# Four banks for the turned blocks of U, 16-bit index look-ups, ten gathered rows a tile in the expert layer of a hybrid decoder

## What is computed

```python
q = (ht @ w_query).reshape(T, 8, 2, 128)
s = einsum('thpd,hpnd->thpn', q, sub_keys)           # 8 heads x 2 halves x 128 keys
top_s, top_i = top_k(s, 16)
cand_s = top_s[:, :, 0, :, None] + top_s[:, :, 1, None, :]      # 16 x 16 sums
cand_i = top_i[:, :, 0, :, None] * 128 + top_i[:, :, 1, None, :]
fin_s, pos = top_k(cand_s.reshape(T, 8, 256), 16)
fin_i = take_along_axis(cand_i.reshape(T, 8, 256), pos, axis=-1)
gate = softmax(fin_s)
act = gelu(einsum('tkd,td->tk', expert_u[fin_i], x))             # 128 experts a token
out = einsum('tk,tkd->td', gate * act, expert_v[fin_i])
```

## Time and profile before

| | |
|---|---|
| median of 3 runs | 3357.28 us (3353.91 to 3363.41) |
| profiled execution | 3359.51 us |
| its span, first to last instruction | 3357.8 us |
| TensorE busy | 3265.7 us (97%) |
| VectorE busy | 2549.1 us (76%) |
| ScalarE busy | 900.3 us (27%) |
| GpSimd busy | 801.7 us (24%) |
| mean granted clock of TensorE | 0.985 of full speed |

### The profile page before, as it was taken

The page is one execution under the profiler, slowest core; times in us unless marked ns, Lnnn a source line. Parts: engine busy times, 40 slices in busy tenths (PEclk is TensorE's granted clock), DMA queues, the critical chain, the costliest instruction groups (busy, mean ns, idle before and its releaser), DMA issues. The chain is left out here.

```text
span 3357.8 us, 46048 instructions
## 1 busy us (share of the span) xinstructions
PE 3265.7 (97%) x17796; PEld 2872.9 (86%) x17796; DVE 2549.1 (76%) x5349; ACT 900.3 (27%) x1310; POOL 801.7 (24%) x625
## 2 busy tenths in 40 slices
PE   8999989899999999999999999999999999999998
PEld 7867755499999999999999999997888888888887
DVE  6611244322499999999989898876999999999996
ACT  4210301111122222224444444432222222222222
POOL 0000000000001100104333333342444444444440
PEclk9999989899999999999999999999999999999999
DMA  3010021311144444448889788889898898988883
GB/s 99 14 40 27 13 88 63 119 57 38 46 133 145 144 141 141 134 137 291 304 308 325 279 324 308 308 320 359 312 318 306 314 314 314 312 318 314 316 309 135
DMA packets 332962, 695.58 MB, mean 207 GB/s; under 512 B 34332, under 2 KB 194936, under 8 KB 326584
## 3 DMA queue, kind: packets, MB, share of 16 engines
q1 hardware_dynamic: 248600, 386.28, 33.0%
q0 software_dynamic: 84144, 306.35, 26.7%
HBM read 580.10 MB, written 110.64 MB: 206 GB/s over the span
## 5 line engine op out<-in xcount | busy, mean ns | idle before, releaser
L1782 ACT ACTIVATE up_a<-up_pa 128x384 f32<-128x384 f32 x256 | 126.0, 492 | 830.8 <-PE up_pa L1767 820.9
L1806 POOL DMA_INDIRECT lead<-in_peer_v_dram,idx x174 | 259.6, 1492 | 352.9 <-DVE acc_s L1825 326.7
L2478 DVE TENSOR_TENSOR acc<-pd_po,acc 128x512 f32<-128x512 f32 x384 | 264.6, 689 | 93.3 <-PE pd_po L2537 90.7
L1806 POOL DMA_INDIRECT gr_row<-in_peer_u_dram,idx x192 | 229.9, 1197 | 368.2 <-DVE raw L1815 341.3
L1815 DVE CUSTOM_DVE_ANT_0 gr_row<-gr_row,xs 128x1024 f32<-128x1024 f32 x192 | 232.1, 1223 | 2.1 <-DMA gr_row<-in_peer_u_dram,idx 2.0
L1806 POOL DMA_INDIRECT dr_row<-in_peer_v_dram,idx x114 | 171.1, 1501 | 215.1 <-DVE acc_s L1825 211.7
L1825 DVE SCALAR_TENSOR_TENSOR acc_s<-lead,gate,acc_s 128x1024 f32<-128x1024 f32 x174 | 222.3, 1278 | 0.0
L2264 DVE TENSOR_SCALAR pg_hot_i<-pg_iota,sel_t 128x128 f32<-128x128 f32 x768 | 214.2, 359 | 0.0
L511 PE MATMUL fr_a<-pj_w,h_t 128*128 128x256 f32 (+1 forms) x864 | 200.3, 394 | 0.9 <-PEq L186 0.9
L2299 PE MATMUL pg_pw<-pg_hot_i,pg_hot_j 128*128 128x128 f32 x1536 | 200.5, 276 | 0.1
L511 PEld LDWEIGHTS fr_a<-pj_w,h_t 128*128 128x128 f32 (+1 forms) x864 | 171.0, 227 | 29.7 <-issue 8.4
(11 more groups left out here) (469 smaller groups left out, 7899.0 us busy)
## 6 DMA issues: line engine op xcount, KB each, us to landing
lead<-in_peer_u_dram SPq DMA_DIRECT2D x128, 512.0 KB, 4.9
room<-in_peer_v_dram SPq DMA_DIRECT2D x128, 512.0 KB, 4.5
act_d<-up_a SPq DMA_DIRECT2D x256, 192.0 KB, 3.5
room<-w_d SPq DMA_DIRECT2D x64, 768.0 KB, 6.6
room<-act_d SPq DMA_DIRECT2D x64, 768.0 KB, 9.2
w_d<-room SPq DMA_DIRECT2D x24, 1024.0 KB, 10.6
w_d<-pg_wb SPq DMA_DIRECT2D x24, 1024.0 KB, 9.0
pj_w<-in_w_in_dram SPq DMA_DIRECT2D x8, 1024.0 KB, 5.7
```

What stands on the lines that cost most here:

```text
L1782: self.nc.scalar.activation(self.a_sb[c][:], self.pa[c][:, 0:WB], ACT.Gelu_apprx_tanh).then_inc(self.a_act, 1)
L1806: pool.indirect_dma_start(self.buf[i % self.n], None, self.table, bass.IndirectOffsetOnAxis(ap=self.idx[:, col:col + 1], axis=0)).then_inc ...
L2478: nc.vector.tensor_tensor(out, po[(OUTS * g + o) % NPO][:], out, ALU.add).then_inc(o_added, 1)
```

## The change

- The transposes of U get four banks of PSUM in place of two: a pair for even and one for odd blocks. The wait of `turn(n, half)` is now for `low(n-2, half)`.
- The look-up runs on 16-bit unsigned integers. The indices and the positions are cast to 16 bits, with the head as the innermost dimension; the compare is laid out with the 16 places outermost and 128 selections innermost. Both halves of the key lie in the buffer `tk_w` (`met`). The sum over 16 places is made by additions of halves: 8, 4, 2, and the last one into 32 bits. Between them stands a `settle()`.
- The constants for the compare are a full array of 16 x 128 (an iota by GpSimd of 2048 elements, before 16).
- ROWS_A_TILE is 10: 80 of the 288 columns are met in the choice, 208 in the gates.
- The gap that aligns the memory stands ahead of the identity matrix of `Up`, not behind it.

```diff
--- before.py
+++ after.py
@@ -1728,7 +1728,10 @@
         self.pa = [ctx.enter_context(nc.psum_tensor(f"up_pa{b}", [P, W4], F32)) for b in range(2)]
 
     def place_turns(self, ctx, nc):
-        self.pt = [ctx.enter_context(nc.psum_tensor(f"up_pt{b}", [P, W4], F32)) for b in range(2)]
+        self.pt = [ctx.enter_context(nc.psum_tensor(f"up_pt{b}", [P, W4], F32)) for b in range(4)]
+
+    def turn_bank(self, n, half):
+        return self.pt[2 * (n % 2) + half]
 
     def load(self, sp, n):
         if n >= 2:
@@ -1750,11 +1753,11 @@
     def turn(self, pe, n, half):
         if half == 0:
             pe.wait_ge(self.u_in[n % 2], 16 * (n // 2 + 1))
-        if n >= 1:
-            pe.wait_ge(self.ut_lo, 2 * (n - 1) + half + 1)
+        if n >= 2:
+            pe.wait_ge(self.ut_lo, 2 * (n - 2) + half + 1)
         for k in range(4):
             c = (4 * half + k) * P
-            mm = self.nc.tensor.transpose(self.pt[half][:, k * P:(k + 1) * P], self.u_sb[n % 2][:, c:c + P], self.ident[:])
+            mm = self.nc.tensor.transpose(self.turn_bank(n, half)[:, k * P:(k + 1) * P], self.u_sb[n % 2][:, c:c + P], self.ident[:])
         mm.then_inc(self.turned, 1)
 
     def up(self, pe, n, c):
@@ -1773,7 +1776,7 @@
             act.wait_ge(self.a_done, 2 * (n - self.NB + 1))
         act.wait_ge(self.turned, 2 * n + half + 1)
         self.nc.scalar.activation(self.ut[n % self.NB][0][:, 4 * half:4 * half + 4, :],
-                                  self.pt[half][:].rearrange("p (k s) -> p k s", k=4), ACT.Copy).then_inc(self.ut_hi, 1)
+                                  self.turn_bank(n, half)[:].rearrange("p (k s) -> p k s", k=4), ACT.Copy).then_inc(self.ut_hi, 1)
 
     def gelu(self, act, n, c):
         act.wait_ge(self.a_done, 2 * n + c + 1)
@@ -1784,7 +1787,7 @@
     def low(self, dve, n, half):
         k = slice(4 * half, 4 * half + 4)
         dve.wait_ge(self.ut_hi, 2 * n + half + 1)
-        self.nc.vector.tensor_tensor(self.ut[n % self.NB][1][:, k, :], self.pt[half][:].rearrange("p (k s) -> p k s", k=4),
+        self.nc.vector.tensor_tensor(self.ut[n % self.NB][1][:, k, :], self.turn_bank(n, half)[:].rearrange("p (k s) -> p k s", k=4),
                                      self.ut[n % self.NB][0][:, k, :].bitcast(F32), ALU.subtract).then_inc(self.ut_lo, 1)
 
 
@@ -1830,7 +1833,7 @@
 UP_TOPK = 7 * NT + 1
 UP_GATES = NK - UP_TOPK
 
-ROWS_A_TILE = 6
+ROWS_A_TILE = 10
 ROWS_TOPK = ROWS_A_TILE * (NT - 1)
 POINTS = 28
 EX_POINT = 20
@@ -1856,12 +1859,15 @@
         w2 = sb("w2", [P, NU, NK])
         top = sb("top", [P, PH, 2, TOPK])
         ids = sb("ids", [P, PH, 2, TOPK], U32)
-        idxf = sb("idxf", [P, PH, 2, TOPK])
+
+        ids_h = sb("ids_h", [P, 2, TOPK, PH], U16)
         fin = sb("fin", [P, PH, TOPK])
         pos = sb("pos", [P, PH, TOPK], U32)
-        pos2 = sb("pos2", [P, 2, PH, TOPK], U32)
-        posf = sb("posf", [P, 2, PH, TOPK])
-        iota = sb("iota", [P, TOPK])
+        pos2 = w2[:].rearrange("p u k -> p (u k)").bitcast(U32)[:, 0:2 * NSEL].rearrange("p (i h k) -> p i h k", i=2, h=PH)
+        pos_h = sb("pos_h", [P, 2, TOPK, PH], U16)
+        places = sb("places", [P, TOPK, PH * TOPK], U16)
+
+        met = w2[:].rearrange("p u k -> p (u k)").bitcast(U16).rearrange("p (i m s) -> p i m s", i=2, m=TOPK)
         res = sb("res", [P, 3, PH, TOPK])
         ex = sb("ex", [P, PH, TOPK])
         sums = sb("sums", [P, PH])
@@ -1881,7 +1887,7 @@
 
         @block.gpsimd
         def _(pool):
-            nc.gpsimd.iota(iota[:], [[1, TOPK]], base=0, channel_multiplier=0,
+            nc.gpsimd.iota(places[:], [[1, TOPK], [0, PH * TOPK]], base=0, channel_multiplier=0,
                            allow_small_or_imprecise_dtypes=True).then_inc(shaped, 1)
             pool.wait_ge(chosen, 1)
             for i in range(ROWS_TOPK):
@@ -1983,7 +1989,6 @@
 
                 w1 = s_sb[:, t]
                 cand, cand2 = (x.rearrange("p u k -> p (u k)").rearrange("p (h k) -> p h k", k=K2) for x in (w1, w2[:]))
-                oh = [x.rearrange("p u k -> p (u k)").rearrange("p (s m) -> p s m", m=TOPK) for x in (w1, w2[:])]
                 units = [(a, i) for a in range(PH) for i in range(2)]
 
                 def key(x, u):
@@ -2014,7 +2019,7 @@
                                     top[:, :, 1, :].unsqueeze(2).broadcast_to([P, PH, TOPK, TOPK]), ALU.add))
                 beside(12)
                 settle()
-                did(v.tensor_copy(idxf[:], ids[:]))
+                did(v.tensor_copy(ids_h[:].rearrange("p i m h -> p h i m"), ids[:]))
                 for a in range(PH):
                     did(v.max(fin[:, a, 0:8], cand[:, a]))
                     if a % 4 == 3:
@@ -2043,25 +2048,30 @@
                 did(v.tensor_scalar(pos2[:, 0], pos[:], 4, None, ALU.logical_shift_right))
                 did(v.tensor_scalar(pos2[:, 1], pos[:], TOPK - 1, None, ALU.bitwise_and))
                 settle()
-                did(v.tensor_copy(posf[:], pos2[:]))
+                did(v.tensor_copy(pos_h[:].rearrange("p i k h -> p i h k"), pos2[:]))
                 beside(21)
                 settle()
                 for i in range(2):
-                    did(v.tensor_tensor(oh[i], iota[:].unsqueeze(1).broadcast_to([P, PH * TOPK, TOPK]),
-                                        posf[:, i].rearrange("p h k -> p (h k)").unsqueeze(2)
-                                        .broadcast_to([P, PH * TOPK, TOPK]), ALU.is_equal))
+                    did(v.tensor_tensor(met[:, i], places[:], pos_h[:, i].rearrange("p k h -> p (k h)").unsqueeze(1)
+                                        .broadcast_to([P, TOPK, PH * TOPK]), ALU.is_equal))
                     beside(22 + i)
                 settle()
                 for i in range(2):
-                    o4 = oh[i].rearrange("p (h k) m -> p h k m", k=TOPK)
-                    did(v.tensor_tensor(o4, o4, idxf[:, :, i, :].unsqueeze(2).broadcast_to([P, PH, TOPK, TOPK]), ALU.mult))
+                    m4 = met[:, i].rearrange("p m (k h) -> p m k h", h=PH)
+                    did(v.tensor_tensor(m4, m4, ids_h[:, i].unsqueeze(2).broadcast_to([P, TOPK, TOPK, PH]), ALU.mult))
                     beside(24 + i)
                 settle()
                 if q > 3:
                     dve.wait_ge(turned, q - 3)
-                for i in range(2):
-                    did(v.tensor_reduce(res[:, i].rearrange("p h k -> p (h k)"), oh[i], AX.X, ALU.add))
-                    beside(26 + i)
+                for n in (8, 4, 2):
+                    did(v.tensor_tensor(met[:, :, 0:n], met[:, :, 0:n], met[:, :, n:2 * n], ALU.add))
+                    if n == 8:
+                        beside(26)
+                    settle()
+                did(v.tensor_tensor(res[:, 0:2].rearrange("p i h k -> p i k h"),
+                                    met[:, :, 0].rearrange("p i (k h) -> p i k h", h=PH),
+                                    met[:, :, 1].rearrange("p i (k h) -> p i k h", h=PH), ALU.add))
+                beside(27)
                 dve.wait_ge(ex_out, q + 1)
                 did(v.tensor_reduce(sums[:], ex[:], AX.X, ALU.add))
                 settle()
@@ -2612,9 +2622,9 @@
             idx = ctx.enter_context(nc.sbuf_tensor("idx", [P, COLS], U32))
             gate = ctx.enter_context(nc.sbuf_tensor("gate", [P, COLS], F32))
             raw = ctx.enter_context(nc.sbuf_tensor("raw", [P, COLS], F32))
+            to_boundary(ctx, nc, "left", 64, boundary=256)
             up = Up(ctx, nc, lead, u_d, act_d)
             turns = ExitStack()
-            to_boundary(ctx, nc, "left", 64, boundary=256)
             with ExitStack() as c1:
                 xs = c1.enter_context(nc.sbuf_tensor("xs", [P, NSP + 1, D], F32))
                 h_d = [c1.enter_context(nc.sbuf_tensor(f"h_d{x}", [P, KD, TD], F32R)) for x in "hl"]
```

## The result

The changed kernel takes 3333.2 us (median of 6 runs, 3330.4 to 3337.2) against 3357.2 us before (6 runs, 3352.3 to 3363.4): a ratio of 0.9928, 95% interval 0.9914 to 0.9942, so 24 us faster. The forecast was 3332 us, 25 us faster. The span of the profiled execution is 3335.0 us, 22.8 us less. The sum was right, but two of its parts were off by some 5 us each, in opposite directions.

| stretch | before | after | difference | forecast |
|---|---|---|---|---|
| start to the choice | 887.9 | 887.4 | -0.5 | 0 |
| choice, to the last transposes | 621.1 | 602.0 | -19.1 | -24.4 |
| gates, to the first product with V | 772.8 | 767.2 | -5.6 | -0.5 |
| product with V and the end | 1076.0 | 1078.3 | +2.3 | 0 |

A forecast was written before the change was run, and what follows sets the result against it. In the choice TensorE and VectorE are both full, VectorE's tile 2.4 us too long. 24.4 us there, 1 from the next stage and half a microsecond less at the boundary give 25 us: 3357.3 to 3332 us, range 3327 to 3340 (0.65).

The forecast's parts named there:

- The sum: Whole kernel: 24.4 us from the choice, 1 from the next stage, half a microsecond less at the boundary: 25 us, 3332 us.
- What bounds the choice: Choice: VectorE's tile, 66.8 us before and 65.5 after, stays longer than TensorE's 64.4 to 64.9; stops move to up(n, 0).
- the low of point 19: Choice: VectorE is 10.8 us behind there in tile 1, 1 us more each tile, passing the tolerated 12 in tile 3.
- Price of a stop before: Choice, TensorE: each of eight stops costs 3.75 us for a wait of 1.94, clock included; 30 us in all.
- the choice's floor: TensorE without stops: last transposes at 1479; as a rival, VectorE's tile under 64.5 us, 3326 us, chance 0.08.
- The look-ups: Choice, VectorE: 16-bit operations at half the 32-bit price, 13.2 to 7.3 us a tile, saving 5.9 us.
- The settles between the additions: VectorE's look-up: three settles at 0.11 us each, 0.35 us a tile, though the Trainium skill says no extra cost.
- The casts: VectorE's look-up: two casts to 16 bits with strided writes, between nothing and 0.13 us each, taken as nothing.
- The end of the choice: VectorE's last step starts at 1484.3 and the last transposes at 1484.6, from 1508.99 before: 24.4 us gain.
- The gates: Stage behind the choice: 32 dots and 32 fetches fewer beside TensorE; gain between 0 and 4.7 us, taken as 1.
- Rows did land in time: Choice: row fetches stay hidden with 2.7 us to spare; rival of rows too late costs 12 us, 3345, chance 0.08.
- The long iota: GpSimd, start of the choice: iota of 2048 elements takes 2 us; costs nothing, at most 1 us.

The follow-up runs named there:

- experiment 2: The whole change, but with six dots a tile in the choice instead of ten: 3329.9 us, ratio 0.9929 to the kernel before.
- experiment 7: The whole change, but with eight dots a tile instead of ten: 3325.9 us, ratio 0.9906 to the kernel before.
- experiment 1: The kernel before with the four banks alone (32-bit look-ups, six dots a tile): 3339.4 us, ratio 0.9953.
- experiment 3: The kernel before with four banks and ten dots a tile, look-ups still in 32 bits: 3376.2 us, ratio 1.0062, slower than before.

## Why the prediction was right, point by point

**What bounds the choice.** Right. With the wait gone TensorE stops where up(n, 0) needs the low of point 19, as forecast, from tile 2 on (tile 3 by the sum). Experiments 2 and 7 show the other side: once VectorE's work for a tile is under 64.8 us the stops are gone.

**Price of a stop before.** Too high. I took 3.75 us for each of eight. The clock fell behind six of them. Behind the first and the seventh the matmuls ran at full speed (timeline of TensorE before; the first row stands just behind the first one of the earlier trace rows):

```profile
1008.68 1.64 PE L1767 MATMUL up_pa<-h_dh,up_ut0h 128*128 128x384 f32 x8
...
1417.79 1.64 PE L1767 MATMUL up_pa<-h_dh,up_ut0h 128*128 128x384 f32 x8
```

These two cost 2.15 us each. So the stops were worth 6 x 3.75 + 2 x 2.15 = 26.8 us and not 30, and the choice's floor is 26.5 us below before (621.1 - 594.6). What the change leaves is 0.77 + 1.61 + 5 x 0.99 = 7.3 us, in agreement with the 7.4 between the change and the floor.

**The look-ups.** The term was right: 2.27 + 2.27 + 2.44 + 0.45 = 7.4 us against 7.3 forecast, and the half price of 16 bits, which no row of before had, is shown (L2055, 1214 ns for 2048 elements; 2.29 us in 32 bits). By the Trainium skill ("VectorE: DVE Perf Modes", The perf-mode tier table) a tensor_tensor on bf16 takes 1224 ns; the trace agrees for 16-bit integers. The settles between the additions cost what the row had shown. The same page says that they cost nothing; the trace disagrees: three additions of 2048, 1024 and 512 elements take 2.44 us until the next starts, where 1.13 + 0.6 + 0.33 = 2.06 stand without settles.

**The casts.** Wrong, small: taken as nothing, with a bound of 0.13 us each. The first costs 0.08 us (the next low starts 1.61 us after the cast's start, before 1.53), the second, with a longer low behind it, 0.37 us. On the other side VectorE's tile before is 66.55 and not 66.8 us. Together 66.55 - 13.2 + 7.4 + 0.45 + 4.6 = 65.8 us, which is what was measured; 65.5 was forecast.

**The end of the choice.** The step that failed most. The sum let the last transposes follow VectorE's last step at once, at 1484.6. VectorE's end came at 1487.1 (mostly by 0.3 us in each of 7.85 tiles), and the transposes at 1489.4, because TensorE was still at its products: behind its last stop (1470.87) it has two blocks of 9.2 us to do, and VectorE only 16.2 us from there to L2088. So the end is TensorE's: its floor of 594.6 us and the 7.3 us that its stops cost. The time that it loses in the middle of the last tile comes on top, whether VectorE is done by then or not. With the choice's start, 0.5 us earlier, this is 5.3 us less gain than forecast.

**The gates.** Here 5.6 us came where I gave 1 within a bound of 4.7. TensorE's waits for the load of U, before and after the change (line, total us, times, longest):

```profile
PE up_pt L1757 <- DMA lead<-in_peer_u_dram: 4.6, 5, 2.2
```

```profile
PE up_pt L1760 <- DMA lead<-in_peer_u_dram: 1.6, 1, 1.6
```

Each of the traces with six dots has gates of 772.8, 769.5 and 772.6 us and 3.2 to 5.9 us of such waits; those with ten dots 765.6 to 769.2 us (seven traces) and 0.8 to 2.3 us of waits. On average that is 4.4 us. A likely cause is the number of fetches that are left for this stage, 208 in place of 240, since they use the DMAs at the same time as the loads of U. It is not shown: the two groups all but touch, and experiments 1 and 3, which differ in the dots alone, have 769.5 and 769.2 us. The bound was too low because it counted idle time alone. In the worst place before, at 1898 us, the time from one turn to the next is 14.29 and 14.45 us on the two sides of a wait of 2.25 us, and 11.87 and 12.77 otherwise: 4.1 us are lost, the part beyond the wait by matmuls that ran slower behind it (eight transposes took 1.69 us, where eight take 1.04), as behind the stops in the choice.

**The rest.** The product with V took 2.3 us longer. This is within what it varies by over the traces, 1075.4 to 1078.4 us. Rows did land in time: they took 5.4 us in the median from issue (4.5 before), but VectorE never waited for one. The long iota took 1.9 us as estimated, and behind VectorE's later first low TensorE waits 1.39 us before the first product, where it waited 1.14 us for a low before: next to nothing, as forecast. The forecast was 25 us by 24.4 + 1 - 0.5; it came out as 19.1 + 5.6 + 0.5 - 2.3. That 3332 and 3333 are so near is luck in part: 5.3 us too much gain in the choice and 5.1 too little in the gates cancelled.

## What to carry to other kernels

When a wait is taken away between two engines that are both over 95% busy, compare their work per round before pricing the gain: the slower one sets the pace, and the wait comes back at the next thing that needs it. Then fill the slack of the other engine to just below the bound's pace and not above it; here ten dots a tile make VectorE the slower one by 1 us in 65, and eight, or nine with turned casts, do not. By the ratios these also lie below six dots, but they did not run beside it, and the intervals of eight and six overlap. Price an instruction by the time to the next start, not by its duration, and a stop by the timeline behind several of its kind.

## What the runs showed of the hardware

- The same idle time had two prices. Of TensorE's eight stops of 1.94 us before the change, six were followed by matmuls at the lower granted clock (2.2 to 2.9 us for the next eight, otherwise 1.64) and two were not. With two banks, ten dots and the light look-ups, stops of 1.0 to 1.4 and of 2.0 us, 11.4 us apart, lowered the clock in one tile of eight (2.32 us for the eight behind, in the others 1.64); with the banks alone six stops of 1.5 to 1.9 us lowered it in none (1.66 to 1.68); in experiment 3 a stop of 2.24 us was free of it and one of 1.90, 11.4 us later, was not. What tells them apart was not tried.
- A cast of 256 elements from 32 to 16 bits with a strided write took 754 ns, 396 with a strided read, and one from 32 to 32 bits in order 294. The two in a tile made it 0.24 us longer than the turned ones, not 0.72.
- VectorE's operations with two 16-bit sources ran at twice the rate of 32 bits also where one source repeats runs of eight elements (L2061, 1214 ns for 2048 elements).
- While VectorE runs long operations with two 32-bit sources a fetch held GpSimd for 2.75 us, and once a tile it still does after the change (2.85 us, beside L2017, the sums); beside a 16-bit compare and beside the 16-bit additions it was 1.68 us, and 0.94 in most other places.
